# Two ScalarE steps of an expert-routing stage moved behind the query and projection copies

## The reference, cut to what matters

```python
def token_block(xt):                       # 128 tokens
    q = (xt @ wq).reshape(128, 8, 2, 128)  # 8 heads, two halves
    s = einsum('thcd,hckd->thck', q, sub_keys)
    top_s, top_i = top_k(s, 16)
    cand = top_s[:, :, 0, :, None] + top_s[:, :, 1, None, :]
    best_s, best_c = top_k(cand.reshape(128, 8, 256), 16)
    expert = i1 * 128 + i2                 # from top_i and best_c
    w = softmax(best_s, axis=-1)
    act = gelu(einsum('thkd,td->thk', u[expert], xt))
    return einsum('thk,thkd->td', w * act, v[expert])
```

## Time and profile before

| what | value |
|---|---|
| median of three executions | 1646.64 us |
| profiled execution, its own time | 1648.42 us |
| its span, first to last instruction | 1646.6 us |
| PE busy | 1429.4 us, 87% |
| DVE busy | 972.0 us, 59% |
| ACT busy | 537.5 us, 33% |
| POOL busy | 510.8 us, 31% |
| DMA queue of the gathers (q0) | 272.63 MB, 42.1% of 16 engines' span |
| DMA queue of the weight chunks (q1) | 138.58 MB, 24.7% |
| granted TensorE clock, mean | 0.988 |

### The profile page before, as it was taken

One profiled execution on the slowest core, in us unless ns is written; L12 is line 12 of the kernel. 1 busy time (PEld: TensorE's weight loads), 2 busy tenths in 40 slices (PEclk: granted clock), 3 DMA queues, 4 the chain that ended last, 5 costly groups with the idle time before them and its releaser, 6 DMA issues. The chain is left out here.

```text
span 1646.6 us, 17356 instructions
## 1 busy us (share of the span) xinstructions
PE 1429.4 (87%) x6624; PEld 943.0 (57%) x6624; DVE 972.0 (59%) x1758; ACT 537.5 (33%) x807; POOL 510.8 (31%) x550
## 2 busy tenths in 40 slices
PE   7999989677777777777777789999999989999998
PEld 6665667222222222222222466668998778689986
DVE  2255488566666667666545643565775365657763
ACT  3253321212121111111113245643443354434432
POOL 4000025767777777777676200000000000000000
PEclk9899999999999999999999999999999999999999
DMA  9323069999999999999999334224553545345543
GB/s 307 119 102 115 3 257 391 404 409 410 409 409 409 409 409 409 409 409 409 410 409 372 134 140 153 102 81 136 193 180 128 195 158 185 104 136 172 180 149 133
DMA packets 162578, 413.75 MB, mean 251 GB/s; under 512 B 11337, under 2 KB 57659, under 8 KB 162368
## 3 DMA queue, kind: packets, MB, share of 16 engines
q0 software_dynamic: 75632, 272.63, 42.1%
q1 hardware_dynamic: 86544, 138.58, 24.7%
q10 hardware_dynamic: 320, 1.43, 0.2%
HBM read 411.55 MB, written 1.05 MB: 251 GB/s over the span
## 5 line engine op out<-in xcount | busy, mean ns | idle before, releaser
L2220 DVE SCALAR_TENSOR_TENSOR arena<-arena,ps 128x1024 f32<-128x1024 f32 x256 | 309.3, 1220 | 224.0 <-DMA arena<-in_peer_u,routes 222.9
L2603 POOL DMA_INDIRECT arena<-in_peer_u,routes x256 | 241.8, 945 | 139.1 <-issue 63.2
L1813 DVE TENSOR_TENSOR w_lo<-ring,w_hi 128x2048 fp32r<-128x2048 f32 x66 | 151.1, 2292 | 103.3 <-ACT w_hi L1653 103.3
L1548 ACT ACTIVATE state<-cst,gatew 128x128 f32<-128x128 f32 x240 | 90.6, 397 | 342.9 <-PE ps L1047 342.8
L1653 ACT ACTIVATE w_hi<-ring 128x2048 fp32r<-128x2048 f32 x66 | 126.3, 1916 | 180.2 <-PE ps L1187 88.3
L1047 PE MATMUL ps<-mixed,state 128*128 128x512 f32 x240 | 118.5, 617 | 39.8 <-ACT state L1548 35.5
L1047 PE MATMUL ps<-wX,state 128*128 128x512 f32 x240 | 117.3, 611 | 40.9 <-DMA wX<-in_peer_v,routes 21.1
L1047 PE MATMUL ps<-xT,state 128*128 128x512 f32 x240 | 117.3, 611 | 39.0 <-ACT state L1548 26.5
L1047 PE MATMUL ps<-proj,state 128*128 128x512 f32 x240 | 117.3, 611 | 37.7 <-DMA proj<-in_peer_v,routes 20.2
L1047 PEld LDWEIGHTS ps<-mixed,state 128*128 128x128 f32 x240 | 41.5, 192 | 116.7 <-ACT state L1548 72.9
L1047 PEld LDWEIGHTS ps<-wX,state 128*128 128x128 f32 x240 | 40.6, 189 | 117.6 <-issue 71.4
(11 more groups left out here) (449 smaller groups left out, 2323.5 us busy)
## 6 DMA issues: line engine op xcount, KB each, us to landing
ring<-in_ffn_w_up SPq DMA_DIRECT2D x22, 2048.0 KB, 8.7
ring<-in_ffn_w_down SPq DMA_DIRECT2D x22, 1024.0 KB, 4.8
ring<-in_even_w_in SPq DMA_DIRECT2D x7, 2048.0 KB, 7.7
ring<-in_w_in SPq DMA_DIRECT2D x6, 2048.0 KB, 11.5
ring<-in_odd_w_in SPq DMA_DIRECT2D x6, 2048.0 KB, 7.7
ring<-in_peer_wq SPq DMA_DIRECT2D x4, 2048.0 KB, 8.7
ring<-in_w_out SPq DMA_DIRECT2D x2, 2048.0 KB, 7.9
arena<-in_peer_u,routes POOLq DMA_INDIRECT x256, 12.6
```

Of the source, the lines that this page charges most:

```text
L1548: do(diags[n % DIAGS], ident, ACT.Copy, scale=gatew[:, u * UROWS + b:u * UROWS + b + 1]).then_inc(diag_ready, 1)
L1813: v.tensor_tensor(w_lo[j % 2][:], w, w_hi[j % 2][:].bitcast(F32), ALU.subtract).then_inc(lo_ready, 1)
L2220: v.scalar_tensor_tensor(row, row, 1.0, token_tile(u // PAIR_UNITS), ALU.mult, ALU.mult, accum_out=dots[:, b:b + 1]).then_inc(u_used, 1)
L2603: pool.indirect_dma_start(arena[:, b % GATHER_SLOTS, :], None, a["peer_u"][0], route_of(u, b))\
```

## The change

The two helpers `logits_exp` and `head_gelu` and their first calls move on ScalarE. Before, `logits_exp(0)` stood after the root of the second tile's norm, and `head_gelu(0, 0)` after the query copy of peer chunk 2. Now both stand after `token_copied(1)`, ahead of the loop over the units. All later calls stay where they were.

```diff
             root("peer1", 1)
-            def logits_exp(u): ...
-            def head_gelu(u, hd): ...
-            logits_exp(0)
             query(1, ps[:, 0, :], slice(0, 1))
...
                 for tt in range(TT):
                     scores_out(c + PAIR_UNITS * tt)
-                if c == 2:
-                    head_gelu(0, 0)
             act.wait_ge(ple_turned, 1)
             do(pT.rearrange("p k t -> p (k t)"), ps[:, 0, :], ACT.Copy).then_inc(pleT_ready, 1)
             act.wait_ge(chunk_done, CHUNK_AT["ple_proj"] + 1)
...
             token_copied(1)
+            def logits_exp(u):
+                part = slice(u * UROWS, (u + 1) * UROWS)
+                act.wait_ge(idx_ready, u + 1)
+                do(gatew[:, part], gatew[:, part], ACT.Exp).then_inc(best_exp, 1)
+            def head_gelu(u, hd):
+                part = slice(u * UROWS + hd * TOPK, u * UROWS + (hd + 1) * TOPK)
+                act.wait_ge(u_used, part.stop)
+                do(dots[:, part], dots[:, part], ACT.Gelu_apprx_tanh).then_inc(gelu_done, 1)
+            logits_exp(0)
+            head_gelu(0, 0)
             for u in range(UNITS):
```

## The result

| | before | changed |
|---|---|---|
| median of 5 executions | 1646.64 us | 1661.19 us |
| lowest, highest | 1644.13, 1648.42 | 1657.05, 1663.93 |
| profiled execution, its own time | 1648.42 us | 1658.09 us |
| its span | 1646.6 us | 1656.3 us |
| ratio, 95% interval | | 1.0085 [1.007, 1.01] |

The ratio is 14 us of 1646.6, with an interval of 11.5 to 16.5. The forecast was 10 us, the median inside its range (1649.5 to 1665). The two profiled executions differ by only 9.7 us, so it has to be found out first what belongs to the change.

The account below looks back on a forecast made before the run. DMA landing of gathers was taken to bound the expert layer. Idle of 8.2 us plus 1.5 for slow restart, say 10, on the 1646.6 us median gave 1656.6 us, 0.6% slower; range 1649.5 to 1665.

Parts of the forecast that it names:

- What bounds the layer: Expert layer: DMA landing of rows sets the pace, 1.28 us per gather; the end moves by DMA idle time, not POOL's.
- The unit period: First gelu of unit 1 to that of unit 2: still 81.9 us; another value would mean the forecast is wrong.
- Nothing is won at the old places: ScalarE's old places of exponential and gelu: both lie in idle time, so removing them makes nothing earlier, 0 us.
- When the exponential comes, and DVE's and POOL's waits: After the token copy: exponential done at 299.17, DVE waits 28.9 us, first gather of unit 1 goes 19.8 us later.
- How much the DMA engines feel: During POOL's pause: 6.6 to 9.7 us idle, taken as 8.2, plus 1.5 for slow restart; together say 10 us.
- The landing of the first gather: Gather 28, first after POOL's pause: lands 5.6 us after issue, at 306.9 us.
- the second way: Check at unit 1's first gelu: gather 28's landing, 34 gathers and a product give 351.6 against 341.8, 9.8 us later.
- What could be late next: Other waits at the start of the interleaved gathers, such as head weights, diagonals and row buffers: all cost nothing.
- When the throughput is full again: DMA throughput after POOL's pause: near zero around 290 to 296 us, full again from about 304.
- The whole pause: Rival: POOL's issue paces the layer, so all 19.8 us are paid, 1666.4 us; chance 0.10.
- Caught up: Rival: leftover transfers fill the gap between the chunk loads, idle only 3 to 4.9 us, around 1650.6; chance 0.13.
- The other side: Rival: POOL's waits for routes in the steady part vanish, winning back 14 us against 10, about 1642; chance 0.03.

Follow-up runs that it names:

- products_early: Kernel before, with DVE making unit 0's products as rows land and unit 1's sums, places and routes later; ratio 0.9983, repeated 0.9985.
- shares_late: Changed kernel, with DVE making unit 0's shares and first head's weights behind product 31 instead of before products 20 and 28; ratio 0.9997.
- gelu_late: Kernel before, with only the first gelu moved behind the token copy; ratio 1.0007.
- exp_mid: Kernel before, with only the exponential moved, less far, to behind the score copies of peer chunk 3; ratio 1.0033.
- hold_before: Kernel before, with SP's load of the second ple_gate_w chunk held until product 31 of unit 0 is done; ratio 1.0015.

## Why the prediction was right, point by point

- *What bounds the layer.* Right. A longer layer and a larger deficit go together to 1.1 us in all runs that slow it, from +0.2 to +23.4 us. The unit period was to stay 81.9 us, and another one was named as a sign of being wrong. It was 82.9 for unit 1 (86.9 to 169.7 us behind the point), against 81.9 in before. So this sign appeared, by 1 us, and with it the other one, a shift at the first gelu that differs from that at the end (11.1 against 12.8). Neither speaks for a rival: the throughput from 330 to 440 us was 409 GB/s in both kernels, and products_early, which has no such pause, also had 82.9. What differs is how long a gather is on its way: near 360 us it landed after 8.4 us in the changed kernel and after 17.8 in before. The shift reached 12.7 at unit 3 and then stayed. Why it came in these steps was not tested.
- *Nothing is won at the old places.* Right: shares_late, with the new order on ScalarE, has 0.9997.
- *When the exponential comes, and DVE's and POOL's waits.* Right to 0.3 us: 29.07 us for DVE and 28.89 us for POOL. Counted from SP's load, the first gather of unit 1 went at 40.5 us (308.92 - 268.38) against 20.4 before (286.53 - 266.14): 20.1 us later, forecast 19.8.
- *How much the DMA engines feel.* The mechanism was right, one term was mis-sized. In stretches of 2 us the deficit against before grew by 2.6 us ahead of the data of the load issued at 285.36, by 6.0 from there to the data of the load of 296.83, and by 3.7 behind that load, together 12.3. Of the 3.7, about 2 us are the empty time before gather 28's data, and the rest is the slow restart. The forecast had 5.0 to 6.4 for the second, 1.6 to 3.3 for the empty time and 1.5 for the restart, all near what was measured, though no row gave the 8 us for which the restart was to last (measured: 306 to 315). The first stood there as zero: "Gather 27 lands at 283.97 as before; the load of 283.1 follows without a gap." Gather 27 landed at 285.4 (17.0 us behind the point, as against 17.8 before), but the load issued at 285.36 had hardly any data moving until 287: 33 and 66 GB/s in the two stretches before. The prediction knew this lead, 7.7 - 5.1 = 2.6 us, and used it for the later load, but left it out here. This is the step that failed, and it is most of the difference between 10 and 12.8.
- *The landing of the first gather.* 5.6 us was taken from the earlier trace rows. Gather 28 landed after 4.1 us, gathers of the steady part near 360 us after 8.4:

```profile
DMA to landing us min/median/max: 4.1/4.1/4.1
```

```profile
DMA to landing us min/median/max: 8.4/8.4/8.4
```

  The 4.1 is what followed from the fit on the Trainium skill's page "DMA: Bandwidth & Descriptors" (section "Anatomy of one DMA — SWDGE (gpsimd) path") with POOL's 0.94 in front; the row that I preferred had other transfers beside it. The page's sum of 8.3 us for the shift was still further off than 9.8: at the first gelu of unit 1 it was 11.1. Both ways counted 34 x 1.28 = 43.5 us from gather 28's landing to the row that releases the gelu, and it took 46.3 (307.7 to 354.0), while landing times grew from 4.1 to 8.4. That the second way gave the same 10 us as the first was therefore luck: the first lacked the hole of 2.6 us, the second took the first landing 1.5 us too long and the service after it 2.8 too short.
- *The table load.* As the row had it, 1.28 us and no drain: the copy ends at 299.91, the load starts at 299.92, the exponential at 301.21. The drain of about 1.38 us that the Trainium skill's page "ScalarE: Activation LUTs" (section "What ACT_TABLE_LOAD costs") counts with each load does not show here.
- *What could be late next.* Right as far as the sum shows, since the deficit of 12.6 us leaves only 0.2 us for other waits. PE waited 19.66 us for the first v row, not for a diagonal. TensorE had run nothing since 296.8 us, and its granted clock was 0.50 (1.2 GHz) from 302 to 318 us. No cost of that shows.
- *When the throughput is full again.* Forecast from about 304 us; it was full only from about 315. Of these 11 us, 2.2 are the later start of the execution.
- *The rivals.* The whole pause (20 us) is ruled out by the changed kernel, by gelu_late and by exp_mid. Caught up (under 4.9) is out by the ratio. The other side came true in its condition and not in its effect: POOL's waits for routes behind 309 us fell from 22.0 us in six waits to 13.6 in four, but the throughput was 409 GB/s with them and without, so nothing was won back.
- *The time.* 1656.6 forecast, 1661.19 measured, 4.6 us more. The layer took 2.8 us more than the 10 forecast. The other 1.8 us lie inside the interval of the ratio (11.5 to 16.5 us, which holds the layer's 12.8), and outside the layer both the start and the rest of the kernel scatter by more than that.

## What to carry to other kernels

Before an activation is moved, look at who consumes it and what stands queued behind that consumer; here twelve products behind one wait held back the gathers, while the late activation itself was free. Where a stage is bound by transfers, price a pause of the issuing engine by the time in which the transfer engines run empty, holes and slow restart included: a pause of 4.7 us cost nothing, one of 29 us cost 12.8. When two traces are compared, count from a point just ahead of the change to one just behind its stage, and only then attribute the difference.

## What the runs showed of the hardware that I had not expected

- After a pause, gathers issued every 1.24 us moved only 312 and 314 GB/s from 306 to 314 us, at a DMA share of 0.90 and 0.89, before they reached 392 and then 416. Added up from 306 to 315 us, this restart cost 2.0 us at the steady rate of 409, beyond the empty time.
- The same shows after a pause in which the engines did not run empty: in hold_before they moved 289 GB/s from 298 to 302 us, at a share of 0.89 and with POOL issuing without a gap since 291.30.
- A gather's time from issue to landing grew from 4.1 us behind the pause to 8.4 near 360 us, and was 17.8 there in before, all at 409 GB/s in the steady part.
- The start of the kernel, up to the point ahead of the change, scattered by 5.7 us between executions, and the stretch behind the layer by 8.2 us (716.5 to 724.7), more than several of the effects studied here; the layer itself took 671.4 us in all three traces with the exponential behind the token copy.
